# Expert weights loaded and given back in order of use, three spare slots, gate rows through memory

## The reference, cut to what matters

```python
for l in range(2):
    mx = jnp.split((silu_c @ w_mod[l] + b_mod[l])[:, None, :], 6, axis=-1)   # mc likewise for context
    ...
    x = x + mx[2] * y_x
    hx = rmsnorm(x, norm_ffn[l]) * (1.0 + mx[4]) + mx[3]
    ...
    x = x + mx[5] * hierarchical_moe(tokens, ...)          # and ctx with mc[5] in layer 0
return rmsnorm(x, norm_final)

def hierarchical_moe(t, ...):      # top-1 of 4 groups, then top-2 of the 8 experts in it
    ...
    hidden = silu(t @ w1_e) * (t @ w3_e)                   # w1, w3: 1024 x 256
    return acc + c_e[:, None] * (hidden @ w2_e)            # w2: 256 x 1024
```

## Time and profile before

| | |
|---|---|
| median of 3 runs | 1144.73 us (1143.92 to 1146.38) |
| profiled execution | 1142.64 us |
| its span, first to last instruction | 1140.6 us |
| TensorE matmuls busy | 976.4 us, 86% |
| VectorE, ScalarE, GpSimd busy | 333.8, 259.5, 235.7 us |
| moved by DMA | 312.66 MB, mean 274 GB/s |
| mean granted TensorE clock | 0.938 |

### The profile page before, as it was taken

The page is one execution under the profiler, slowest core; times in us unless marked ns, Lnnn a source line. Parts: engine busy times, 40 slices in busy tenths (PEclk is TensorE's granted clock), DMA queues, the critical chain, the costliest instruction groups (busy, mean ns, idle before and its releaser), DMA issues.

```text
span 1140.6 us, 17923 instructions
## 1 busy us (share of the span) xinstructions
PE 976.4 (86%) x5993; PEld 640.8 (56%) x5994; DVE 333.8 (29%) x720; ACT 259.5 (23%) x539; POOL 235.7 (21%) x331
## 2 busy tenths in 40 slices
PE   3999998989996998888998399999959989878881
PEld 2444475457884555555555175878845555555550
DVE  2169953542165110000100361255170101000103
ACT  3111023452131221111221230223122212111212
POOL 1118010100123132323231100000123323223310
PEclk9999999999997998998998799999978989998986
DMA  9992235994259799999999793232054999999972
GB/s 370 289 315 74 74 88 207 380 352 184 74 175 342 262 402 406 408 408 406 356 408 400 268 348 114 74 111 89 23 203 151 399 404 387 409 405 405 403 281 111
DMA packets 126899, 312.66 MB, mean 274 GB/s; under 512 B 28567, under 2 KB 59543, under 8 KB 126068
## 3 DMA queue, kind: packets, MB, share of 16 engines
q1 hardware_dynamic: 101488, 285.63, 66.5%
q10 hardware_dynamic: 14628, 13.53, 3.8%
q0 software_dynamic: 10720, 12.64, 3.2%
HBM read 312.49 MB, written 21.76 MB: 293 GB/s over the span
## 4 chain that ended last, share of the span: by engine, by line
PE 59%; DMA 26%; DVE 6%; ACT 3%; SPq 2%; issue 2%; ACTq 1%; POOL 0%; POOLq 0%; DVEq 0%
DMA ring<-in_moe_w 22%; PE ps L700 17%; PE ps L814 12%; PE ps L840 5%; PE ps L710 5%; PE ps L1005 4%; PE ps L636 3%; PE ps L1130 2%; SPq L572 2%; PE ps L667 1%; DMA PR<-in_odd_conv 1%; PE ps L792 1%; PE ps L683 1%; PE ps L729 1%; DMA RT<-pair_out 1%
## 5 line engine op out<-in xcount | busy, mean ns | idle before, releaser
L814 PE MATMUL ps<-ring,RT 128*64 128x256 f32 x2144 | 280.8, 420 | 59.7 <-DMA ring<-in_moe_w 56.7
L814 PEld LDWEIGHTS ps<-ring,RT 128*64 128x64 f32 x2144 | 186.1, 152 | 132.3 <-issue 68.2
L700 PE MATMUL ps<-RT,ring 128*128 128x512 f32 (+1 forms) x576 | 196.1, 500 | 1.0 <-ACT RT L1382 1.0
L700 PEld LDWEIGHTS ps<-RT,ring 128*128 128x128 f32 x576 | 109.4, 192 | 84.9 <-issue 76.6
L840 PE MATMUL ps<-ring,RT 128*64 128x512 f32 x536 | 127.8, 593 | 1.9 <-DVE RT L1771 1.1
L1754 DVE TENSOR_TENSOR RT<-RT,ps 64x256 f32<-64x256 f32 x64 | 27.0, 423 | 337.8 <-ACT RT L1332 337.8
L1332 ACT ACTIVATE RT<-ps 64x256 f32<-64x256 f32 x64 | 24.2, 378 | 300.1 <-PE ps L814 300.1
L1831 DVE SCALAR_TENSOR_TENSOR RAB<-RM,chan,RAB 128x512 f32<-128x512 f32 x120 | 79.7, 746 | 0.0
L2073 POOL DMA_INDIRECT RH<-hrow,sidx_all x64 | 67.5, 1055 | 55.8 <-POOL sidx_all L2070 55.8
L2085 POOL DMA_INDIRECT pair_out<-RH,sidx_all x64 | 65.3, 1021 | 59.0 <-POOL sidx_all L2082 54.7
L2050 POOL TENSOR_TENSOR X<-X,PR 128x512 f32<-128x512 f32 x12 | 15.2, 1266 | 270.8 <-DVE PR L1639 270.8
(11 more groups left out here) (229 smaller groups left out, 938.1 us busy)
## 6 DMA issues: line engine op xcount, KB each, us to landing
ring<-in_moe_w SPq DMA_DIRECT2D x384, 512.0 KB, 13.4
ring<-in_w_mod SPq DMA_DIRECT2D x96, 512.0 KB, 9.0
ring<-in_odd_w_in SPq DMA_DIRECT2D x24, 512.0 KB, 9.0
ring<-in_even_w_in SPq DMA_DIRECT2D x20, 512.0 KB, 10.2
ring<-in_even_w_out SPq DMA_DIRECT2D x8, 512.0 KB, 11.9
RT<-pair_out ACTq DMA_DIRECT2D x4, 1024.0 KB, 5.9
ring<-in_odd_w_out SPq DMA_DIRECT2D x8, 512.0 KB, 9.5
hrow<-RH ACTq DMA_DIRECT2D x6, 512.0 KB, 8.3
```

Of the source, the lines that this page charges most:

```text
L700: mm = pe.matmul(bank, w[:, c, P * ft:P * (ft + 1)], moving[:, c, :], start=(c == 0), stop=(c == NCH - 1))
L814: mm = pe.matmul(bank[CAP * k:CAP * (k + 1), 0:BLK], xt(c), w[k][:, BLK * c:BLK * (c + 1)], start=(c == 0), stop=(c == NCH - 1))
```

## The change

It reorders how expert weights are loaded and released, and takes the experts' gate rows another way.

- A piece (w1, w3 or w2 of one expert) is released as soon as it has been used: w1 and w3 after `U(q)` and `more(q)`, w2 after `Dn(q)`. SP loads in that order: w1 and w3 of q, then w2 of q-1.
- The first group puts w1 and w3 of expert 3 and w2 of expert 2 into three spare slots, `RAB` (two) and `G` (one), loaded once `h_ready` has come. A layer's experts then take 93 ring slots, and the releases of w2 of expert 1 and of w1 and w3 of expert 3 are not counted (`HELD`), which keeps releases in the order of slots.
- `step(q)` is now `T(q+1)`, `Hd(q-1)`, `U(q)`, `more(q)`, `Dn(q-1)`: the same order of steps under another name, but the extra block comes before `Dn(q-1)`. ScalarE, VectorE and GpSimd follow, and the first group is unrolled on all of them.
- The wait for drained banks before the experts is taken bank by bank.
- `G` is busy as a spare slot, so the gate vector of the experts isn't broadcast by TensorE and drained by ScalarE. ScalarE stores the row of `modrow` to memory (`store_gate`), and SP reads it back broadcast over the partitions, behind the last expert weight.

```diff
@@ -234,11 +231,28 @@
 
     at, n = {}, 0
     for name, slots in (("mod0a", 8), ("in0", 10), ("mod", 24), ("mod12", 4), ("out0", 4), ("mod13", 4), ("mod14", 8),
-                        ("moe0", 3 * EXPERTS), ("in1", 12), ("out1", 4), ("moe1", 3 * EXPERTS)):
+                        ("moe0", MOE_SLOTS), ("in1", 12), ("out1", 4), ("moe1", MOE_SLOTS)):
         at[name] = n
         n += slots
     return at
 
+
+
+SPARE = {(3, 0): 0, (3, 1): 1, (2, 2): 2}
+HELD = [(1, 2), (3, 0), (3, 1)]
+MOE_SLOTS = 3 * EXPERTS - len(SPARE)
+FIRST = {(0, 0): 0, (0, 1): 1, (1, 0): 2, (1, 1): 3, (0, 2): 4, (2, 0): 5, (2, 1): 6, (1, 2): 7, (3, 2): 10}
+LAST_GROUP = EXPERTS // PER_LOOP - 1
+
+
+def ring_place(base, i, q, k):
+
+    if isinstance(i, int) and i == 0 and (q, k) in FIRST:
+        return base + FIRST[q, k]
+    if k < 2:
+        return base + 3 * q - 4 + k
+    final = isinstance(i, int) and (i, q) == (LAST_GROUP, PER_LOOP - 1)
+    return base + 3 * q + 1 - (2 if final else 0)
 
 
...
@@ -323,6 +337,8 @@
         CV = BIASF[:, 512:1536].rearrange("p (c t) -> p c t", c=4)
         OD = PR[:, :, :].rearrange("p a b -> p (a b)").rearrange("p (n d) -> p n d", n=8)
 
+        spare = [RAB[:, 0:2048], RAB[:, 2048:4096], G[:, :, :].rearrange("p s d -> p (s d)")]
...
         dve_drained = sem("dve_drained")
         landed = [sem(f"landed{i}") for i in range(RING)]
         ring_free = sem("ring_free")
+        spare_landed = [sem(f"spare_landed{k}") for k in range(3)]
+        gate_stored, ld_gate = sem("gate_stored"), sem("ld_gate")
         ld_const, ld_x, ld_ctx, ld_c, ld_bmod, ld_rows, ld_grow, ld_router, ld_lam, ld_rot, ld_final = (
...
@@ -557,21 +576,55 @@
             def experts(l):
                 base = at[f"moe{l}"]
                 assert slots_filled[0] == base
-                with sp.Fori(0, EXPERTS // PER_LOOP) as i:
+
+                def weight(slot, landing, i, q, k):
+                    e = i * PER_LOOP + q
+                    one = slice(e, e + 1) if isinstance(e, int) else bass.ds(e, 1)
+                    w = A[("moe_w1", "moe_w3", "moe_w2")[k]][l, one, :, :]
+                    for a in (0, 1):
+                        if k < 2:
+                            src = w[:, 512 * a:512 * (a + 1), :].rearrange("e (p j) n -> p (e j n)", j=4)
+                        else:
+                            src = w.rearrange("e (p f) n -> p f (e n)", p=P)[:, a, :]
+                        sp.dma_start(slot[:, 1024 * a:1024 * (a + 1)], src).then_inc(landing, 16)
+
+                def in_ring(i, q, k):
+                    s = ring_place(base, i, q, k)
+                    sp.wait_ge(ring_free, i * RING + (s - RING + 1))
+                    weight(ring[:, s % RING, :], landed[s % RING], i, q, k)
+
+                def in_spare():
+                    for parity in (0, 1):
+                        sp.wait_ge(h_ready[parity], (2, 3)[l])
+                    for (q, k), n in SPARE.items():
+                        weight(spare[n], spare_landed[n], 0, q, k)
+
+                for q, k in ((0, 0), (0, 1), (1, 0), (1, 1), (0, 2), (2, 0), (2, 1), (1, 2)):
+                    in_ring(0, q, k)
+                if l == 0:
+                    in_spare()
+                in_ring(1, 0, 0)
+                in_ring(1, 0, 1)
+                in_ring(0, 3, 2)
+                in_ring(1, 1, 0)
+                if l == 1:
+                    in_spare()
+                in_ring(1, 1, 1)
+                in_ring(1, 0, 2)
+                for q in (2, 3):
+                    in_ring(1, q, 0)
+                    in_ring(1, q, 1)
+                    in_ring(1, q - 1, 2)
+                with sp.Fori(2, LAST_GROUP + 1) as i:
                     for q in range(PER_LOOP):
-                        for k, name in enumerate(("moe_w1", "moe_w3", "moe_w2")):
-                            n = base + 3 * q + k
-
-                            sp.wait_ge(ring_free, i * RING + (n - RING + 1))
-                            w = A[name][l, bass.ds(i * PER_LOOP + q, 1), :, :]
-                            for a in (0, 1):
-                                if k < 2:
-                                    src = w[:, 512 * a:512 * (a + 1), :].rearrange("e (p j) n -> p (e j n)", j=4)
-                                else:
-                                    src = w.rearrange("e (p f) n -> p f (e n)", p=P)[:, a, :]
...
@@ -778,9 +831,9 @@
             def experts(l):
                 n0, base = EXPERTS * l, at[f"moe{l}"]
 
-                end = plan["slots", l, 1]["n"]
-                for name in list(plan)[end - BANKS + 1:end + 1]:
-                    drained(pe, *name)
+                def emptied(bank):
+                    names = list(plan)[:plan["slots", l, 1]["n"] + 1]
+                    drained(pe, *[n for n in names if plan[n]["bank"] <= bank < plan[n]["bank"] + plan[n]["wide"]][-1])
...
-                def wait_slot(i, q, k):
-                    s = base + 3 * q + k
-                    pe.wait_ge(landed[s % RING], (i + (s // RING + 1)) * 32)
+                def weight(i, q, k, wait=True):
+                    if isinstance(i, int) and i == 0 and (q, k) in SPARE:
+                        n = SPARE[q, k]
+                        if wait:
+                            pe.wait_ge(spare_landed[n], 32 * (l + 1))
+                        return spare[n]
+                    s = ring_place(base, i, q, k)
+                    if wait:
+                        pe.wait_ge(landed[s % RING], (i + (s // RING + 1)) * 32)
                     return ring[:, s % RING, :]
...
@@ -840,11 +899,12 @@
                             mm = pe.matmul(bank[CAP * k:CAP * (k + 1), :], ht(f),
                                            w[:, D * f + 512 * k:D * f + 512 * (k + 1)],
                                            start=(f == 0), stop=(f == 1))
+                            freed(mm)
                     return mm
 
-                def more(q, count):
-
-                    w = [ring[:, (base + 3 * q + k) % RING, :] for k in range(3)]
+                def more(i, q, count):
+
+                    w = [weight(i, q, k, wait=False) for k in (0, 1)]
                     bank = ps[:, 7, :]
                     with pe.If(count > 0):
                         with pe.Fori(0, count):
...
-                            down(w[2], lambda f: HTX[:, f, :], bank).then_inc(x_y_full, 1)
-
-                def step(i, q, count, ahead2=True, ahead1=True):
-
-
-                    if ahead2:
-                        T(*job_after(i, q, 2))
-                    Hd(i, q)
-                    if ahead1:
-                        U(*job_after(i, q, 1))
-                    Dn(i, q)
-                    more(q, count)
-                    free(3)
-
+                            down(weight(i, q, 2), lambda f: HTX[:, f, :], bank).then_inc(x_y_full, 1)
+
+                def used(i, q, ks):
+                    first = isinstance(i, int) and i == 0
+
+                    free(sum(not (first and (q, k) in HELD) for k in ks))
+
+                def step(i, q, count, ahead=True):
+
+                    if ahead:
+                        T(*job_after(i, q, 1))
+                    Hd(i, q - 1)
+                    U(i, q)
+                    more(i, q, count)
+                    used(i, q, (0, 1))
+                    Dn(i, q - 1)
+                    used(i, q - 1, (2,))
+
+                emptied(0)
                 T(0, 0, start=(l == 0))
+                emptied(1)
                 T(0, 1, start=(l == 0))
+                emptied(2)
                 U(0, 0, start=(l == 0))
+                for bank in range(3, BANKS):
+                    emptied(bank)
                 pe.wait_ge(extra_ready, l + 1)
 
-                last = EXPERTS // PER_LOOP - 1
                 c = extra_counts(pe, l, 0)
-                for q in range(PER_LOOP):
+                more(0, 0, c[0])
+                used(0, 0, (0, 1))
+                for q in range(1, PER_LOOP):
                     step(0, q, c[q])
-                with pe.Fori(1, last) as i:
+                with pe.Fori(1, LAST_GROUP) as i:
                     c = extra_counts(pe, l, i)
                     for q in range(PER_LOOP):
                         step(i, q, c[q])
-                c = extra_counts(pe, l, last)
+                c = extra_counts(pe, l, LAST_GROUP)
                 for q in range(PER_LOOP):
-                    step(last, q, c[q], ahead2=(q < 2), ahead1=(q < 3))
+                    step(LAST_GROUP, q, c[q], ahead=(q < PER_LOOP - 1))
+                Hd(LAST_GROUP, PER_LOOP - 1)
+                Dn(LAST_GROUP, PER_LOOP - 1)
+                used(LAST_GROUP, PER_LOOP - 1, (2,))
 
                 pe.wait_ge(y_ready, n0 + EXPERTS)
                 pe.wait_ge(x_y_ready, pe.snap(extras))
...
@@ -1011,7 +1084,6 @@
                 free(1)
             rows(1, "scale", 4)
             rows(1, "shift", 3)
-            rows(1, "gate", 5)
...
@@ -1189,6 +1260,11 @@
                         name = "norm_mix" if v == 1 else "norm_ffn"
```

(28 more changed lines are left out.)

66 lines of the change are left out of this document (39 added, 27 removed).

## The result

| | before | after |
|---|---|---|
| median | 1144.56 us (1143.92 to 1146.38, 4 runs) | 1123.97 us (1123.26 to 1125.05, 4 runs) |
| ratio, 95% interval | | 0.9818 (0.9801 to 0.9835) |
| profiled execution, its span | 1142.64, 1140.6 us | 1124.22, 1122.5 us |
| mean granted TensorE clock | 0.938 | 0.932 |

A forecast was written before the change was run, and what follows sets the result against it. Both expert stages were taken as bound by DMA weight bytes, with time won from idle DMA engines and the tail. Layer 0's 13.7 us and layer 1's 16.3 took 30 us off, giving 1114.5 us; range 1105 to 1128, 0.73 for 1105 to 1122.

The forecast's parts named there:

- rival 1: Half the gain comes: layer 0 gives 6 us through contention, layer 1 11; 17 us in all, 1127.7 us; chance 0.18.
- Three spare slots: Expert weights land in layer 1's idle stretch before its experts, 7.7 us won; in layer 0 they carry the engines over 361 to 366.
- Release after use: w1 and w3 of expert 0 are released after `U(0)`, 6.8 us earlier in layer 1, less 2.0 us for withheld releases.
- order of use: At each stage's end w3(31) is loaded one slot earlier, so `U(31)` starts sooner: 2.6 us a stage, possibly only 1.
- dents: Short DMA idle stretches in the expert stages go: 2.8 us in layer 0 at 547 to 560, 0.9 and 0.3 in layer 1.
- gate rows: Taking the gate matmuls off TensorE gains 0.2 us in layer 0, where VectorE is in the norm, and 0 in layer 1.
- Layer 0's front: Idle DMA time from 361 to 401, 10.1 us, comes back, less 2 us for expert 1's extra block and withheld releases, bounds 0 and 5.
- no dent of 0.8 in either stage: Sign in the profile after: no such fall of DMA share in the expert stages, but a small one where releases are withheld.
- The rule against it: Fuller weight queue at 361 to 366 delays first gathers and the lambda row: `U(0)` of layer 0 up to 4 us later, 1118.7.
- What is moved: `more(q)` before `Dn(q-1)` waits for w2(q): priced at 0, at most 3 us for each of three extra blocks.
- Read back of G: Behind the last expert weight, a broadcast load at 3.6 us, hidden by some 19 us; without that cover 2.6 us.
- TensorE becomes the bound: In layer 1's expert stage matmuls would outlast the weight bytes, needing 23 us of new waits; about 1135 us, chance 0.03.

The follow-up runs named there:

- gate_alone: The kernel before with only the gate rows taken through memory, ring, release and order as before; 1148.91 us against 1143.23, ratio 1.0056.
- no_spares: The changed kernel without the three spare slots, ring of 12, same order of use and release; 1135.29 us, ratio 0.9924 to the kernel before.
- gate_filler: gate_alone plus matmuls of no use, eight in layer 0 where the gate matmuls stood and nine before layer 1's transposes; ratio 0.9966 to the kernel before.
- late_spares: The changed kernel with layer 0's three spare slots requested behind the first `U`, no filler; 1121.30 us, ratio 0.9809 to the kernel before.
- filler_l0: The changed kernel with eight matmuls of no use in the old place of layer 0's gate matmuls; ratio 0.9960 to the kernel before.

## Why the prediction was right in the whole and wrong in some of its steps

The time was in the range, 9.5 us above the forecast value. It was outside 1105 to 1122, which had the 0.73; it lies in the part of the range that was added for rival 1, and what put it there was not rival 1's cause. The expert stages came out near the sum (28.6 of 29.8 us, 2.4 of them by a shortening that gate_alone has too and that no term of the sum contains), and that the whole stayed in the range owes something to luck. By its own steps:

**Three spare slots.** Forecast 7.7 us in layer 1, less 2.0 for the withheld slots: 5.7. Measured 4.9 or 4.3 there, by the execution of the changed kernel, and 4.6 or 6.4 in layer 0, withheld slots included. Mechanism right, in layer 1 some 1 us too large.

**Release after use, order of use, dents.** no_spares has these and the gate rows through memory, so the kernel to compare with is gate_alone, which differs from it in these and in the wait for drained banks, taken bank by bank. Layer 1: forecast 6.8 + 0.9 + 0.3 + 2.6 = 10.6, measured 254.3 - 246.6 = 7.7. Against the kernel before it would be 10.1, but that takes in the 2.4 us by which gate_alone's stage is shorter. Layer 0: forecast 10.1 - 7.7 + 2.8 + 2.6 = 7.8, measured 267.9 - 260.3 = 7.6. After a release, layer 1's first `U` ends at 859.8 and SyncE issues at 860.17, as written down for it. The first `U` of layer 1 that waits for weights starts at 984.2, 130 us into the stage, where it was 904.6, 47 us into it. `U(31)` starts at 1090.5, not at 1077: 7.5 + 1.1 + 1.9 of these 13.5 us are the later start of what lies in front of it. From the start of `U(31)` to the last `Dn` it is now 6.2 us (1090.51 to 1096.67) where it was 7.8 (1106.92 to 1114.76). That isn't the new order: `U(31)` itself took 5.36 us at a granted clock of 0.68 and now takes 3.67 at 1.00, and gate_alone, in the old order, has 6.2 us too. The 2.6 us of the order by themselves were measured in no run.

**The step that failed most: gate rows.** "It stood on the chain, but the next use of its result is a transpose that VectorE copies ... I book 0.2 us", and 0 for layer 1. The wait was read rightly; what a wait does to TensorE was not. I asked who waits for the result of the removed matmuls and not what the engine would do in their place. In place of the 0.2 the runs put a loss of 7.2 us at layer 0's front, and 5.7 (medians) to 6.2 us (spans) for this part alone in gate_alone; other matmuls in the same place cure it (gate_filler). The 0 for layer 1 is not shown to be wrong: front 1 is 2.0 us longer in gate_alone, but the wait in front of its slow router matmuls is in the kernel before as well. The warning was in the trace of the kernel before: from 352 to 362, behind a wait of 2.9 us at 351.2, its windows have a clock of 0.62 and then 0.50.

**Layer 0's front.** "I take 2 us lost again, bounds 0 and 5": the extra block of expert 1 did leave a hole, share 0.72 from 380 to 400, as in the kernel before. That share against 1.03 is 6 us, outside the 0 to 5, and the sign "no dent of 0.8 in either stage" failed here. late_spares closes the hole (1.03 there), but its stage, 255.6 us, is no shorter, since with three slots fewer in front it is idle earlier: share 0.48 from 353 to 362, where the changed kernel has 1.03. From 335 to 410 both move the same, 340 GB/s. So in the changed kernel most of what the spares carried ahead was lost again at the hole.

**The rule against it.** That the lambda row's result "is waited for in front of the first `copy_xT`" was the right place, priced at up to 4 us. In the changed kernel its load took 4.9 us and the first `U` paid little. With a warm clock it is 10 us more (14.8 against 4.5) and 20 at the first `U`. The Trainium skill, page DMA: Bandwidth & Descriptors, section Issuing engines are not separate DMA queues, says that DMAs of all engines run interleaved on the same 16 DMA engines, and the trace agrees. It adds that the time to initiate a DMA is usually small relative to the DMA itself. Beside a full queue it isn't small in this case: 7.62 us for the issue of a 2 KB load.

**What is moved.** Priced at 0, and nearly so: in stage 0 TensorE waited 0.7 us in all for a w2.

**Read back of G.** Hidden, as forecast, though not by its price: in layer 0 it took up to 16.3 us to land, not 3.6, behind weights issued just before, and was issued at 610.7 and 611.9 for a use at 642.6.

**Sum.** In spans, kernel by kernel: the gate rows cost 6.2 us (1140.6 to 1146.8, gate_alone), order and release gain 13.3 (to 1133.5, no_spares), the spares 11.0 (to 1122.5), in all 18.1. By the stages alone it is 15.3 for order and release and 9.5 to 10.7 for the spares. Each term is from single executions: front 1 alone differs by 3.3 us between two executions of the same kernel (21.9 and 18.6), and the times of a kernel's executions lie up to 7.6 us apart on a chip.

Rival 1, half of the gain, came nearest in size by its end (17 us) and wrongly in cause. Its own terms give more than it says: 7.7 + 6.8 + 0.9 + 0.3 - 3.4 + 1 is 13.3 for layer 1, not 11, and 19.3 in all. That TensorE becomes the bound and that gathers do are both off the table: TensorE still waited 19.5 us for weights in stage 0 (28.9 before).

## What to carry to other kernels

Before work is taken off TensorE, look at what it does in the time set free: if it then waits, the matmuls behind the wait may run at half the clock, and if they are on the chain the saving turns into a loss. Move needed work into the gap. And before more is queued ahead of a hand-over between stages, list every small load that any engine issues and waits for there: load those rows before the queue is filled, or request the extra slots after the hand-over. When a repair makes things worse, look for a second fault that the first had hidden before dropping the theory.

## What the runs showed of the hardware

- A 3.07 us wait of TensorE, after 16 us of nearly unbroken matmuls at 1.00, was followed by a granted clock of 0.50 (1.2 GHz) from 335.7 to 356, though TensorE was busy for all of these 20.3 us. The same transposes and router matmuls, begun without the wait, ran at 1.00 to their end (gate_filler, 335.3 to 349). The Trainium skill, page TensorE: Matmul & The Clock Gate, section HAM oscillation, describes waits for DMA that leave the next matmuls slow; the trace agrees that a wait does this; here it was one for VectorE.
- A wait doesn't always do it: in layer 1 both executions of the changed kernel wait 4.07 us before the transposes, and the 32 router matmuls take 6.88 us in one and 4.01 in the other:

```profile
832.50 6.88 PE L782 MATMUL ps<-WR,RT 128*128 128x36 f32 x32
```

```profile
835.13 4.01 PE L782 MATMUL ps<-WR,RT 128*128 128x36 f32 x32
```

- A ScalarE DMA issue took 0.45 to 0.65 us where the DMA engines had room (late_spares, from 358.9 on), and up to 7.62 us beside a full weight queue (filler_l0); no other instruction of ScalarE started meanwhile.
